# Two fused transformer layers on one core: steps spread over batches by TensorE's work, a gate chunk ahead of attention, meta tokens in one product, first keys in two parts

## The chip, the core and the metric

One core of a Trainium2 chip runs the whole program in one launch. The metric is the device time of that launch in microseconds (us), over several runs. Engines are named as in the profile: PE (TensorE), PEld (its weight loads), DVE (VectorE), ACT (ScalarE), POOL (GpSimd), SP (SyncE, which issues the plain DMAs). All arithmetic is float32.

## What is computed

Two layers over 512 tokens of width 1024, 16 learned meta tokens ahead of them in the first layer. In short:

```python
a = rmsnorm([meta, x], w)                       # 528 rows
aq, ak, av, rq, rf, ri, rg = split(a @ w_in)    # 7 x 512 columns
att = diff_attention(aq, ak, av)                # 4 heads, 2 softmaxes each, causal
rec = hgrn2(rq, rf, ri, rg)                     # gated recurrence, 4 heads, gated by silu(rg)
h = x + [att, rec] @ w_out
# per token: 8 heads; scores against 2 x 128 keys, top 16 of the 16 x 16 sums -> 128 experts
hid = gelu(u_table[experts] @ rmsnorm(h)) * softmax(scores)
h = rmsnorm(h + hid @ v_table[experts])
# second layer: stick-breaking attention (8 heads) and a spatial gate, gated sum, w_out, norm
```

A pair of expert rows (one of `u`, one of `v`) is 2 x 4 KB; 512 tokens x 128 experts make 537 MB of gathers, beside 201 MB of weights and inputs.

## The kernel before

**Blocks.** The tokens are four blocks of 128. The first layer's mixing runs for blocks (0), (1) and (2, 3); the second layer for (0, 1), (2) and (3).

**Gathers and batches.** POOL issues 512 indirect DMAs (line 1804), each of 128 pairs of rows (1.05 MB), into a ring of eight buffers `uv_rows`. A batch ("tick") is two gathers; there are 256, 64 to a block. In each, DVE multiplies the u halves with the tokens (`dots`, line 1618, two instructions), ACT applies gelu (`gelu`), DVE makes the weights (`mix`, lines 1627 and 1628), and PE adds the weighted v halves into the two banks `py` (`rows`: 4 products in the program, 8 records in the trace). Only `rows` frees the two buffers (`uv_free`), for which POOL waits. The ring is thus four ticks deep.

**Order of the work.** `make_plan` writes one list of steps, PLAN, and every engine walks it in order, doing its part of each step. First comes all that block 0 needs before its first gather (`first`), then the 256 ticks, then block 3's second layer. Into the ticks, `spread` deals the rows of the other blocks' work: row r of n goes to tick `lo + r * (hi - lo) // n`, whatever it costs. A row is a list of steps that stand together: of projections two tiles (one where the group has two blocks), of attention one stage each of two heads (`pipeline`). In PE's list `rows` of tick k-1 stands behind the steps of tick k.

**Steps that matter here.** `rf`, `rq`, `ak`, `aq` are tiles of a product with columns as the result (`cols_tile`: 8 products, 512 KB of weights); `ri`, `av`, `rg`, `out` and most of the second layer have rows as the result (`rows_tile`: 4 tiles to a chunk, whose PSUM banks stay open until the fourth). `wq` (4 tiles) and `sc` make the scores of two heads of the expert lookup, `tk` is their top-16 on DVE in six parts. Attention of a head: `us` (scores), `ue` (exponentials on ACT), `uw` (weights on DVE), `ut` (transposes), `uv` (values). `lx`, `ly`, `lm` are the levels of the recurrence: DVE differences and ACT exponentials, DVE products, PE products. `zs` to `zv` are the second layer's attention, `zb` and `za` its gates. PSUM: three banks `pa`, three `pb`, two `py`. Weights go through four slots `wbuf`, loaded by SP in PLAN's order as slots come free (`load_tile`).

**Keys before.** For heads 2i, 2i+1 of block b, `keys` puts the five steps at one tick, 5 ahead of the need, and hands out up to two or four a tick where no chunk is open and no scores wait.

**Meta tokens before.** For group (0) the 16 meta columns lie in `aT_meta`, apart; `cols_tile` makes 8 products of 128 columns and then 8 of 16 columns for the tiles of `rf` and `ak`.

**Constants before.** SP issues x, the angles, meta and 15 constants ahead of the first weights; all constants count on one semaphore `ld_c`, for which `rows_to_columns(0)`, `lambdas` and `norm1` wait.

Of the kernel before, what the change touches and what calls it, by code (L numbers as in the profile page):

```python
# [14 lines left out]
P = 128  # L15
D = 1024
# [97 lines left out]
def mixing_rows(g):  # L114
# [4 lines left out]
    if g == (0,):  # L119
        rows[0].append(("lam",))  # L120
# [4 lines left out]
    rows += second + [[("fq", g)]]  # L125
    proj = tiles("ri", g) + tiles("ak", g) + tiles("av", g) + tiles("aq", g)
# [4 lines left out]
    else:  # L131
# [24 lines left out]
def key_steps(b, i):  # L156
    return [("wq", b, i, t) for t in range(4)] + [("sc", b, i)]
# [67 lines left out]
def use(s):  # L225
# [12 lines left out]
    if name in ("ua", "ud"):  # L238
# [5 lines left out]
            "xt": (2, 0, 0), "sc": (1, 0, 1), "n3": (0, 2, 0), "zs": (0, 1, 0), "zt": (1, 0, 0), "zv": (1, 0, 0),  # L244
# [28 lines left out]

def make_plan():
# [11 lines left out]
    keys = {}  # L286
    for b in range(NB):
        for i in range(4):
            slot = PER_HEAD * (HP * b + 2 * i - LEAD)
            if slot > 0:  # L290
                keys[slot - 5] = ([("xt", b)] if (b, i) == (3, 0) else []) + key_steps(b, i)
    out, pending, chunk = [], [], Open()
    for k in range(n):
# [6 lines left out]
        pending += keys.get(k, [])  # L300
        room = 2 if len(pending) > 2 else 4
        for s in [None] + ticks[k]:
            if s:
                out.append(s)
                chunk.add(s)
            while pending and room and not chunk.now():
                out.append(pending.pop(0))
                room -= 1
# [4 lines left out]
    assert not pending  # L313
# [54 lines left out]
def build(nc, t, out):  # L368

    ctx = ExitStack()  # L370
    with ctx:
# [113 lines left out]
        aT_meta = cut(aT_words[:, KT * P:KT * P + KT * NM], KT, NM)  # L485
# [111 lines left out]
        def _(sp):  # L597
# [38 lines left out]
            for s in PLAN:  # L636
# [28 lines left out]
                if use(s)[2]:  # L665
                    load_tile()
# [1249 lines left out]
```

## Time and profile before

| | us |
|---|---|
| median of 3 runs | 2182.97 (2171.31 to 2190.44) |
| profiled execution, its own time | 2175.92 |
| its span | 2174.1 |
| PE busy | 1750.3 (81%) |
| DVE busy | 1323.0 (61%) |
| ACT busy | 640.2 (29%) |
| POOL busy | 574.5 (26%) |

The span is the time from the first to the last instruction of the profiled execution; 1.8 us of its time lie around it. Busy shares are means over stages that differ: there are no gathers in the first 205 us nor in the last 160, and in between PE is busy all of some stretches and little over half of others. Bytes moved in a stretch, in GB/s, tell how near the transfers are to what they reach elsewhere in the same execution.

### The profile page before, as it was taken

Reading aid. Unit: us, or ns where it says so; the run is one execution under the profiler, and the core shown is the slowest. Engines: PE = TensorE matmul, PEld = TensorE weight load, DVE = VectorE, ACT = ScalarE, POOL = GpSimd, SP = SyncE. Lnnn points to the kernel's source line nnn. Section 1 sums busy time; section 2 is a strip of 40 time slices with the busy share of each in tenths; the row PEclk is TensorE's granted clock in tenths of the full one; section 3 lists DMA queues with packets and bytes.
Section 4 is the critical chain, followed back from the end, with each engine's and each line's share of the span. In section 5 each row is a group of like instructions: output and inputs, shape, how many; then the busy total and the mean of one; then the engine's idle time right before and its main releaser. Section 6 shows DMA issues by size and latency. Waiting matters only on the chain.

```text
span 2174.1 us, 20766 instructions
## 1 busy us (share of the span) xinstructions
PE 1750.3 (81%) x7102; PEld 883.9 (41%) x7102; DVE 1323.0 (61%) x3450; ACT 640.2 (29%) x1233; POOL 574.5 (26%) x516
## 2 busy tenths in 40 slices
PE   7975788768898786887565999889996886777897
PEld 5744454316464342433122635353434342222553
DVE  2324678766778646667777457766566577744231
ACT  3121423322443233302014113621213145311361
POOL 0001224332322222224443222333333333422000
PEclk9977899888999877797886999899997997999899
DMA  5426999998998756699999999899999999999665
GB/s 177 145 64 217 377 411 415 372 417 342 412 394 332 277 227 259 262 418 393 421 420 363 379 397 374 315 355 417 416 379 401 417 416 400 387 417 412 216 212 183
DMA packets 132906, 739.59 MB, mean 340 GB/s; under 512 B 15793, under 2 KB 17201, under 8 KB 67265
## 3 DMA queue, kind: packets, MB, share of 16 engines
q0 software_dynamic: 73728, 536.90, 61.1%
q1 hardware_dynamic: 59072, 201.36, 25.1%
q8 instruction: 57, 0.93, 0.2%
q14 instruction: 49, 0.39, 0.1%
HBM read 736.11 MB, written 2.10 MB: 340 GB/s over the span
## 4 chain that ended last, share of the span: by engine, by line
PE 48%; DMA 28%; DVE 13%; ACT 5%; issue 4%; POOL 2%; SPq 0%; POOLq 0%; DVEq 0%
PE pa L695 28%; DMA uv_rows<-in_peer_uv,small 17%; DMA wbuf<-in_wt 11%; PE py L695 10%; PE pb L695 8%; DVE uv_rows L1618 4%; POOL uv_rows L1804 2%; ACT area L1057 2%; ACT L1053 1%; DVE small L1527 1%; ACT an L1057 1%; DVE tk L1628 1%; DVE small L1605 1%; PE pb L731 1%; ACT small L1057 0%
## 5 line engine op out<-in xcount | busy, mean ns | idle before, releaser
L1804 POOL DMA_INDIRECT uv_rows<-in_peer_uv,small x512 | 574.3, 1122 | 1428.8 <-PE py L695 1135.3
L1618 DVE CUSTOM_DVE_ANT_0 uv_rows<-uv_rows,xrep 128x1024 f32<-128x1024 f32 x512 | 617.5, 1222 | 299.6 <-DMA uv_rows<-in_peer_uv,small 299.1
L695 PE MATMUL py<-uv_rows,tk 128*64 128x512 f32 x2048 | 575.3, 690 | 135.1 <-DVE tk L1628 134.7
L695 PE MATMUL pa<-wbuf,area 128*128 128x512 f32 (+1 forms) x800 | 377.7, 616 | 45.8 <-DMA wbuf<-in_wt 31.6
L1057 ACT ACTIVATE small<-small 128x2 f32<-128x2 f32 (+3 forms) x324 | 69.1, 214 | 1003.4 <-DVE small L1618 993.2
L695 PEld LDWEIGHTS py<-uv_rows,tk 128*64 128x64 f32 x2048 | 138.8, 152 | 459.7 <-issue 251.8
L695 PEld LDWEIGHTS pa<-wbuf,area 128*128 128x128 f32 (+1 forms) x800 | 144.0, 191 | 264.8 <-issue 209.2
L695 PE MATMUL pa<-area,wbuf 128*128 128x128 f32 (+2 forms) x1280 | 202.5, 317 | 8.1 <-DMA wbuf<-in_wt 4.6
L695 PEld LDWEIGHTS pa<-area,wbuf 128*128 128x128 f32 x1280 | 180.7, 199 | 40.0 <-issue 18.6
L695 PE MATMUL pb<-wbuf,area 128*128 128x512 f32 x352 | 168.1, 622 | 22.9 <-DMA wbuf<-in_wt 15.1
L1057 ACT ACT_TABLE_LOAD x137 | 175.8, 1283 | 28.4 <-PE pa L695 20.0
L1057 ACT ACTIVATE area<-pa 128x512 f32<-128x512 f32 (+7 forms) x227 | 87.0, 406 | 221.6 <-PE pa L695 205.2
L695 PE MATMUL pa<-xnT,wbuf 128*128 128x128 f32 x1024 | 130.3, 287 | 25.6 <-DMA wbuf<-in_wt 8.5
L1053 ACT ACT_TABLE_LOAD x101 | 129.6, 1283 | 62.9 <-DVE area L1420 47.0
L695 PEld LDWEIGHTS pa<-xnT,wbuf 128*128 128x128 f32 x1024 | 123.7, 200 | 50.3 <-issue 31.2
L695 PE MATMUL pa<-area 128*128 128x128 f32 (+7 forms) x408 | 99.6, 383 | 39.1 <-ACT area L1057 26.6
L695 PEld LDWEIGHTS pb<-wbuf,area 128*128 128x128 f32 x352 | 65.3, 195 | 123.3 <-issue 82.1
L695 PEld LDWEIGHTS pa<-area 128*128 128x128 f32 (+2 forms) x408 | 66.3, 231 | 79.8 <-ACT area L1057 41.3
L695 PE MATMUL pb<-area 128*128 128x128 f32 (+7 forms) x434 | 79.6, 324 | 3.3 <-DVE area L1431 1.4
L1628 DVE TENSOR_TENSOR tk<-small,tk 128x128 f32<-128x128 f32 x256 | 74.9, 293 | 8.9
L1627 DVE TENSOR_TENSOR tk<-small 128x2 f32<-128x2 f32 x256 | 41.1, 161 | 61.1 <-PE py L695 41.0
L1057 ACT ACTIVATE area<-area 128x512 f32<-128x512 f32 (+3 forms) x104 | 67.4, 655 | 19.4 <-DVE area L1420 14.4
(198 smaller groups left out, 1195.0 us busy)
## 6 DMA issues: line engine op xcount, KB each, us to landing
wbuf<-in_wt SPq DMA_DIRECT2D x352, 512.0 KB, 7.9
uv_rows<-in_peer_uv,small POOLq DMA_INDIRECT x512, 11.3
wbuf<-in_skT SPq DMA_DIRECT2D x16, 256.0 KB, 7.3
h<-in_x SPq DMA_DIRECT2D x4, 512.0 KB, 11.6
fw<-in_finw SPq DMA_DIRECT2D x4, 512.0 KB, 11.3
out<-h SPq DMA_DIRECT2D x4, 512.0 KB, 6.0
an<-in_x SPq DMA_DIRECT2D x3, 512.0 KB, 6.1
uv_rows<-in_finw SPq DMA_DIRECT2D x2, 512.0 KB, 6.0
```

The lines of the kernel that those rows point to most:

```text
L695: return nc.tensor.matmul(o, l, r, start=start, stop=stop, skip_group_check=True)
L731: last = nc.tensor.transpose(ps[:, P * k:P * (k + 1)], src[:, P * (4 * h + k):P * (4 * h + k + 1)], ident)
L1053: nc.scalar.preload_act_table_set("natural_log_exp_and_others")
L1057: return nc.scalar.activation(dst, src, func, **more)
L1527: last = V.tensor_reduce(mx[:, q, part:part + 1], psum_a[(first + part) % RA][:, 0:nk - lo], AXX, ALU.max)
L1605: V.tensor_scalar(gate[to, cols], gexps[tok, g % 2, s_::TG], gsum[tok, g % 2, 1:2], None, ALU.mult)
L1618: last = V.tensor_tensor_reduce(uv_rows[:, n % RING, 0:D], uv_rows[:, n % RING, 0:D], xrep[:, b % 2, n % TG, :], 1.0, 0.0, ALU.mult, ALU.a ...
L1627: step(V.tensor_tensor(wcol[:, k % 2, :], dots[:, at:at + BATCH], gate[:, col:col + BATCH], ALU.mult))
L1628: V.tensor_tensor(mix_w[k % 2], token_mask.unsqueeze(1).broadcast_to([P, BATCH, TOK]), wcol[:, k % 2, :].unsqueeze(2).broadcast_to([P, BAT ...
L1804: nc.gpsimd.indirect_dma_start(uv_rows[:, n % RING, :], None, t["peer_uv"], bass.IndirectOffsetOnAxis(ap=expert_ids[:, c:c + 1].bitcast(U3 ...
```

## The change

1. **Spread by work.** `spread` weighs each row by `tensor_work` (at least `LEAST` = 2) and places its middle in proportion; no two rows share a tick while there is room. The ranges are a little longer: blocks 2 and 3's mixing by 4 ticks, the second layer of (0, 1) ends 4 ticks later.
2. **Keys placed one by one.** `place_keys` walks each key step through a window of up to 16 ticks ahead of its need and takes the tick with least PE work in which no chunk is open and no scores wait.
3. **Gate chunk.** For (2, 3) the four tiles of `rg` stand ahead of attention, not in its first two rows.
4. **Meta tokens.** The 16 meta columns lie behind the 128 in one operand; a tile of `rf` or `ak` is 8 products of 144 columns.
5. **First keys in two parts.** For heads 0 and 1 `sc` becomes two steps `s1`, each behind two `wq`, and `tk` of head 0 waits for the first alone.
6. **Constants.** Only `ident` and `normw` are loaded ahead of the weights, on a semaphore of their own; the others and the angles follow the fourth `rf` tile; `lam` stands with the first `rq` row.

```diff
@@ mixing_rows
-    second[0] = second[0] + [("fs", g)]
+    second[0] = second[0] + [("lam",)] * (g == (0,)) + [("fs", g)]
...
-        rows += weave(chain, proj) + [[("rotq", g)]]
+        rows += weave(chain, proj) + [[("rotq", g)] + rg[0:1]] + pairs_of(rg[1:], n)
...
-    att[0] = att[0] + rg[0:1]
-    att[1] = att[1] + rg[1:4]
+    if len(g) == 1:
+        att[0] = att[0] + rg[0:1]
+        att[1] = att[1] + rg[1:4]
@@ key_steps
+    if (b, i) == (0, 0):
+        return [s for h in range(2) for s in (("wq", b, i, 2 * h), ("wq", b, i, 2 * h + 1), ("s1", b, i, h))]
@@ spread
-    for r, row in enumerate(rows):
-        ticks[lo + r * (hi - lo) // len(rows)] += row
+    work = [max(LEAST, sum(map(tensor_work, row))) for row in rows]
+    done, at = 0, lo - 1
+    for row, w in zip(rows, work):
+        at = min(at + 1, lo + int((done + w / 2) * (hi - lo) / sum(work)))
+        ticks[at] += row
+        done += w
@@ place_keys
+            lo = max(last, inputs_at.get(b, 0) + 1, need - 2 * PER_HEAD + 1)
+            for j, s in enumerate(steps):
+                end = lo + max(1, (need - lo) // (len(steps) - j))
+                spots = [k for k in range(lo, end) if gaps[k]] or [k for k in range(lo, len(ticks)) if gaps[k]][:1]
+                k = min(spots, key=lambda k: work[k])
@@ make_plan
-    spread(mixing_rows((2, 3)) + input_rows(2) + [[("xt", 2)]], q3, PER_BLOCK + q3, ticks)
+    spread(mixing_rows((2, 3)) + input_rows(2) + [[("xt", 2)]], q3, PER_BLOCK + q3 + 4, ticks)
-    spread(second_rows((0, 1)), 2 * PER_BLOCK + 6, 3 * PER_BLOCK + 10, ticks)
-    spread(second_rows((2,)), 3 * PER_BLOCK + 10, n, ticks)
+    spread(second_rows((0, 1)), 2 * PER_BLOCK + 6, 3 * PER_BLOCK + 14, ticks)
+    spread(second_rows((2,)), 3 * PER_BLOCK + 14, n, ticks)
@@ sync
+                if s == ("rf", (0,), 3):
+                    for name, dst in CONSTS:
...
+                    load_angles((0,))
@@ cols_tile
-                    last = mm(ps[:, 0:n], w[:, k, :], src[:, k, :], k == 0, k == KT - 1)
-                for k in range(KT if meta is not None else 0):
-                    last = mm(ps[:, n:n + NM], w[:, k, :], meta[:, k, :], k == 0, k == KT - 1)
+                    last = mm(ps[:, 0:n], w[:, k, :], src[:, k, 0:n], k == 0, k == KT - 1)
```

On PE, at the start of the program (behind the transposes of the inputs): the last two `rf` tiles, `rq` and the first `ri` tile, before

```order
L695 MATMUL pa<-area,wbuf 128x128 x8
L695 MATMUL pa<-area,wbuf 128x16 x8
L695 MATMUL pa<-area,wbuf 128x128 x8
L695 MATMUL pa<-area,wbuf 128x16 x8
L695 MATMUL pa<-area,wbuf 128x128 x32
L695 MATMUL pa<-wbuf,area 128x512 x2
L695 MATMUL pa<-wbuf,area 16x512 x2
```

and now, from the transposes on:

```order
L800 MATMUL pb<-ident,uv_rows 128x16 x8
L788 MATMUL pb<-ident,an 128x128 x8
L754 MATMUL pa<-area,wbuf 128x144 x32
L754 MATMUL pa<-area,wbuf 128x128 x32
L754 MATMUL pa<-wbuf,area 128x512 x2
L754 MATMUL pa<-wbuf,area 16x512 x2
```

The 32 products of 16 columns of `rf` are gone, and its 32 products of 128 columns have 144.

On PE, where attention of block 2 begins (`pa<-area 128x400` are scores, `pa<-wbuf,area 128x512` tiles of `rg`, `xnT` a `wq` tile, `py` is `rows`), before

```order
L695 MATMUL pb<-area 128x512 x2
L695 MATMUL py<-uv_rows,tk 64x512 x4
L695 MATMUL pa<-area 128x400
L695 MATMUL pa<-tri,ident 128x128
L695 MATMUL pa<-area 128x400
L695 MATMUL pa<-tri,ident 128x128
L695 MATMUL pa<-wbuf,area 128x512 x4
L695 MATMUL py<-uv_rows,tk 64x512 x4
L695 MATMUL pa<-wbuf,area 128x512 x12
L695 MATMUL pa<-xnT,wbuf 128x128 x16
L695 MATMUL py<-uv_rows,tk 64x512 x4
L695 MATMUL pa<-xnT,wbuf 128x128 x16
```

and now

```order
L754 MATMUL pb<-area 128x512 x2
L754 MATMUL pa<-wbuf,area 128x512 x4
L754 MATMUL py<-uv_rows,tk 64x512 x4
L754 MATMUL pa<-wbuf,area 128x512 x4
L754 MATMUL py<-uv_rows,tk 64x512 x4
L754 MATMUL pa<-wbuf,area 128x512 x4
L754 MATMUL py<-uv_rows,tk 64x512 x4
L754 MATMUL pa<-wbuf,area 128x512 x4
L754 MATMUL py<-uv_rows,tk 64x512 x4
L754 MATMUL pa<-area 128x400
L754 MATMUL pa<-tri,ident 128x128
L754 MATMUL pa<-area 128x400
```

One `rg` tile stands between two `rows` where three stood with two `wq` tiles, and the scores follow the chunk.

On PE, at the `zb` chunk of the second layer of (0, 1), before

```order
L695 MATMUL pa<-xnT,wbuf 128x128 x16
L695 MATMUL pa<-wbuf,area 128x512 x8
L695 MATMUL py<-uv_rows,tk 64x512 x4
L695 MATMUL pa<-wbuf,area 128x512 x4
L695 MATMUL py<-uv_rows,tk 64x512 x4
L695 MATMUL pa<-wbuf,area 128x512 x4
L695 MATMUL pa<-xnT,wbuf 128x128 x16
```

and now

```order
L754 MATMUL pa<-wbuf,area 128x512 x4
L754 MATMUL py<-uv_rows,tk 64x512 x4
L754 MATMUL pa<-ident,xrep 128x64 x16
L754 MATMUL pa<-xnT,wbuf 128x128 x8
L754 MATMUL pb<-area 128x64 x16
L754 MATMUL py<-uv_rows,tk 64x512 x4
```

The tiles of the chunk stand one to a tick, without key steps; ahead of the attention that follows there now stand `xt` (`ident,xrep`), one `wq` and `sg` (`pb<-area 128x64`) in one tick, where before it `za`'s four tiles stood in one.

## Rows read from the trace of the kernel before

**Rows 1.** The page, part 2: GB/s in 40 equal slices of the span.
```profile
GB/s 177 145 64 217 377 411 415 372 417 342 412 394 332 277 227 259 262 418 393 421 420 363 379 397 374 315 355 417 416 379 401 417 416 400 387 417 412 216 212 183
```

**Rows 2.** Windows where the second layer's tiles already stand one a tick.
```profile
1250.00:1275.00 25.00, 25.00 (x72) 9.02 (x71) 16.48 (x47) 4.88 (x10) 7.61 (x8) 1.00 1.02 419
```

**Rows 3.** Windows: us; busy of PE, PEld, DVE, ACT, POOL; clock; DMA share; GB/s.
```profile
234.00:500.00 266.00, 211.47 (x964) 109.61 (x963) 195.01 (x524) 82.88 (x165) 85.84 (x78) 0.88 0.98 400
500.00:725.00 225.00, 201.52 (x926) 117.91 (x928) 174.41 (x463) 81.63 (x134) 72.66 (x66) 0.94 0.94 368
725.00:775.00 50.00, 37.51 (x138) 19.02 (x140) 19.47 (x48) 10.46 (x21) 7.55 (x7) 0.80 0.67 249
775.00:900.00 125.00, 87.87 (x291) 40.36 (x292) 79.07 (x220) 42.89 (x108) 29.95 (x27) 0.71 0.57 214
...
1175.00:1275.00 100.00, 93.77 (x379) 52.84 (x378) 59.10 (x168) 19.41 (x45) 26.89 (x28) 0.94 0.94 371
1275.00:1475.00 200.00, 180.04 (x720) 89.23 (x719) 132.95 (x329) 78.03 (x130) 58.40 (x53) 0.92 0.91 355
1475.00:1825.00 350.00, 299.15 (x1136) 132.81 (x1136) 230.98 (x612) 97.01 (x184) 116.01 (x100) 0.95 1.00 409
```

**Rows 4.** Timeline of the first keys: `wq` and `sc` on PE, top-16 on DVE, first gather.
```profile
183.59 9.05 PE L695 MATMUL pa<-xnT,wbuf 128*128 128x128 f32 x64 [0.69 <-ACT xnT L1057]
193.00 1.16 PE L695 MATMUL pa<-wbuf,qp 128*128 128x128 f32 x8 [0.37 <-ACT qp L1057]
...
194.83 0.29 DVE L1566 MAX8 tk<-sc 128x8 f32<-128x128 f32 x1 [21.23 <-ACT sc L1057]
...
205.62 1.07 POOL L1804 DMA_INDIRECT uv_rows<-in_peer_uv,small  x1 [205.17 <-DVE small L1606]
```

**Rows 5.** Timeline of PE and POOL where the `rg` chunk runs: start, us, [idle before].
```profile
744.10 6.73 PE L695 MATMUL pa<-wbuf,area 128*128 128x512 f32 x8 [8.27 <-ACT area L1057]
...
752.63 10.57 PE L695 MATMUL pa<-wbuf,area 128*128 128x512 f32 x24
...
752.98 0.94 POOL L1804 DMA_INDIRECT uv_rows<-in_peer_uv,small  x1 [22.62 <-PE py L695]
...
763.03 3.73 PE L695 MATMUL pa<-xnT,wbuf 128*128 128x128 f32 x32
```

**Rows 6.** Timeline of PE around the `za` chunk of the second layer.
```profile
1343.11 1.94 PE L695 MATMUL py<-uv_rows,tk 128*64 128x512 f32 x8
...
1348.22 13.90 PE L695 MATMUL pa<-wbuf,area 128*128 128x512 f32 x32
1362.05 1.94 PE L695 MATMUL py<-uv_rows,tk 128*64 128x512 f32 x8
```

**Rows 7.** Windows of `py` alone (x counts its records, 8 a tick), attention of blocks 2, 3.
```profile
775.00:909.00 134.00, 40.26 (x128) 9.66 (x128) 0.00 (x0) 0.73 0.60 227
```

**Rows 8.** Timeline inside that attention, one head of block 3.
```profile
861.05 1.29 DVE L1527 TENSOR_REDUCE small<-pa 128x1 f32<-128x512 f32 x2 [4.59 <-PE pa L695]
...
868.38 0.20 ACT L1057 ACTIVATE small<-small 128x2 f32<-128x2 f32 x1 [10.05 <-DVE small L1618]
...
870.82 0.37 PE L830 MATMUL pa<-ident,area 128*16 128x128 f32 x1 [7.94 <-ACT area L1057]
```

**Rows 9.** Groups by shape, PE, 17.5 to 101 us (x records, two to a product | busy us, mean ns).
```profile
L695 PE MATMUL pa<-area,wbuf 128*128 128x128 f32 x248 | 31.9, 287 | 0.9 <-DVE area L1380 0.9
...
L695 PE MATMUL pa<-area,wbuf 128*128 128x16 f32 x128 | 15.3, 261 | 0.0
```

**Rows 10.** Timeline of the start: PE's first wait, then two levels of the recurrence.
```profile
13.34 1.03 PE L743 MATMUL pb<-ident,uv_rows 16*128 16x16 f32 x8 [13.34 <-DMA small<-in_bs]
...
57.23 2.05 PE L695 MATMUL pb<-area 128*128 128x128 f32 x16
...
64.20 0.42 DVE L1431 TENSOR_TENSOR area<-area 128x256 f32<-128x256 f32 x1
...
69.76 2.03 PE L695 MATMUL pb<-area 128*128 128x128 f32 x16
```

More of the change, by code:

```diff
@@ L271, in add, with place_keys @@
             self.scores = s[0] == "us"
+def place_keys(ticks):
+    chunk, gaps = Open(), []
+    for row in ticks:
+        free = [] if chunk.now() else [0]
+        for i, s in enumerate(row):
+            chunk.add(s)
+            free += [] if chunk.now() else [i + 1]
+        gaps.append(free[:1])
+    work = [sum(map(tensor_work, row)) for row in ticks]
+    inputs_at = {s[1]: k for k, row in enumerate(ticks) for s in row if s[0] == "xt"}
+    inputs_at[0] = 0
+    chosen, last = [[] for _ in ticks], 0
+    for b in range(NB):
+        for i in range(4):
+            need = PER_HEAD * (HP * b + 2 * i - LEAD) - 1
+            if need < 0:
+                continue
+            steps = ([("xt", b)] if (b, i) == (3, 0) else []) + key_steps(b, i)
+            lo = max(last, inputs_at.get(b, 0) + 1, need - 2 * PER_HEAD + 1)
[3 more added lines that the diff above has]
+                k = min(spots, key=lambda k: work[k])
+                chosen[k].append(s)
+                work[k] += tensor_work(s)
+                lo = k
+            last = lo
+    for k, steps in enumerate(chosen):
+        if steps:
+            ticks[k][gaps[k][0]:gaps[k][0]] = steps
 def make_plan():
@@ L281, in make_plan @@
     spread(mixing_rows((1,)) + input_rows(1) + [[("xt", 1)]], 0, q3, ticks)
-    spread(mixing_rows((2, 3)) + input_rows(2) + [[("xt", 2)]], q3, PER_BLOCK + q3, ticks)
+    spread(mixing_rows((2, 3)) + input_rows(2) + [[("xt", 2)]], q3, PER_BLOCK + q3 + 4, ticks)
     spread([[("ldpost",)], *input_rows(3), [("ldfin1",)]], 2 * PER_BLOCK, 2 * PER_BLOCK + 5, ticks)
-    spread(second_rows((0, 1)), 2 * PER_BLOCK + 6, 3 * PER_BLOCK + 10, ticks)
-    spread(second_rows((2,)), 3 * PER_BLOCK + 10, n, ticks)
[L286 to L292, printed above, removed]
+    spread(second_rows((0, 1)), 2 * PER_BLOCK + 6, 3 * PER_BLOCK + 14, ticks)
+    spread(second_rows((2,)), 3 * PER_BLOCK + 14, n, ticks)
+    place_keys(ticks)
+    out = []
     for k in range(n):
@@ L299, in make_plan @@
             out.append(("take", b - 1))
[L300 to L308, printed above, removed]
+        out += ticks[k]
         g = k // PER_HEAD + LEAD
@@ L710, in rows_tile @@
                     open_banks.clear()
-                    open_banks.extend(bank() for _ in range(len(g) + (meta is not None)))
+                    open_banks.extend(bank() for _ in range(len(g) + meta))
                 for j, ps in enumerate(open_banks):
@@ L717, in rows_tile @@
                         else:
-                            last = mm(ps[0:NM, :], meta[:, 2 * i + k, :], w[:, k, :], i + k == 0, i == n_tiles - 1 and k == 1)
+                            last = mm(ps[0:NM, :], src[:, k0 + 2 * i + k, P * len(g):], w[:, k, :], i + k == 0, i == n_tiles - 1 and k == 1)
                     if i == n_tiles - 1:
@@ L735, in rows_to_columns @@
                 if b == 0:
[L736 removed]
+                    pe.wait_ge(ld_i, LOADED_F)
                     rows[0] += 1
@@ L865, in key_scores, with head_scores @@
                 last.then_inc(a_full, 1)
+            def head_scores(b, i, h):
+                pe.wait_ge(a_free, A_AT[("wq", b, i, 2 * h + 1)])
+                sk = cut(tile()[:, 0:2 * P], 2, P)
+                ps = a_bank()
+                for k in range(2):
+                    last = mm(ps[:, P * k:P * (k + 1)], qp[:, 2 * h + k, :], sk[:, k, :], True, True)
+                last.then_inc(a_full, 1)
             def weighted_rows(k):
@@ L1277, in _ @@
                     empty(qp[:, s[3], :], bank()[:, 0:P])
+                elif name == "s1":
+                    empty(sc[:, 0, 2 * P * s[3]:2 * P * (s[3] + 1)], bank()[:, 0:2 * P])
                 elif name == "sc":
```

76 lines of the change are left out of this document (49 added, 27 removed).

## The prediction

> **What bounds the kernel now.** I read the bytes per slice first, then the stretches one by one, then the timeline where a stretch falls short.
>
> The slices show a plateau: 15 of the 33 between the first and the last gather stand at 400 to 421 GB/s, and a valley of five stands at 227 to 332 [rows 1]. A stretch of 25 us at 419 GB/s has a DMA share of 1.02, that is, the transfers are never idle there [rows 2]. I take 418 GB/s as what the transfers reach. What a stretch misses of it is time in which they had nothing to do, and as the bytes are fixed (537 MB of gathers, 201 MB besides), only that time can be won between the gathers. It is us x (1 - GB/s / 418) [rows 3]:
>
> - 234 to 500: 266 x 18/418 = 11.5 us
> - 500 to 725: 225 x 50/418 = 26.9 us
> - 725 to 775: 50 x 169/418 = 20.2 us
> - 775 to 900: 125 x 204/418 = 61.0 us
> - 1175 to 1275: 100 x 47/418 = 11.2 us
> - 1275 to 1475: 200 x 63/418 = 30.1 us
> - 1475 to 1825: 350 x 9/418 = 7.5 us
>
> Together 168 us. The other part is the start, where no gather runs until 205.6 us [rows 4]: there PE and the chains between engines set the pace.
>
> Why the transfers pause: a gather needs a free buffer, and only `rows` frees one. The longest waits of POOL are for `py` (22.6 us before the gather at 753) [rows 5]. So a tick in which PE, in its order, does long work ahead of `rows` empties the ring of four ticks.
>
> **The change, part by part.**
>
> *Gate chunk.* At 744.1 PE runs the first `rg` tile at the lower clock (6.7 us), one `rows`, then three tiles (10.6 us) and two `wq` tiles (3.7 us) ahead of the next `rows` [rows 5]. From 744 to 767 the ring gets two buffers back in 23 us. Before that the first tile waited 8.3 us for the exponentials to free a bank. In the changed order one tile (10.57 / 3 = 3.5 us) stands between two `rows` (1.9 us [rows 6]): 5.4 us a tick, under the (2.10 + 0.52 MB) / 418 = 6.3 us that a tick's transfers take. Of 20.2 us I leave 3 for the entry of the chunk: **-17**. Bounds: 0 (the wait at `us20` stays and merely moves) and -20.
>
> *Attention of blocks 2 and 3.* From 775 to 909, 128 records of `py` are 16 ticks in 134 us, 8.4 us a tick, against 2.10 / 418 = 5.0 us for the gathers of one [rows 7]. The cause is a chain, not work: DVE's maxima wait 4.6 us for PE's scores, ACT's gelu waits 10.1 us for the dots behind them, PE's transposes wait 7.9 us for the exponentials, and `rows` stands behind these [rows 8]. The change leaves this chain as it is. But its 18 rows lie in 18 ticks (79 to 96), where they lay in 17 (74 to 90), with four `wq` and one `sc` among them (2.36 MB). If the chain takes its 134 us again, it hides 18 x 2.10 + 2.36 = 40.1 MB where 134 x 227 GB/s = 30.4 MB passed: 9.7 MB, 23 us. The key steps each take a bank and an ACT copy inside the chain, so I take **-21**. Bounds: 0 (each key step lengthens the chain by what it hides) and -45 (the higher clock, since PE idles less, also shortens the scores).
>
> *Second layer of (0, 1).* The four `za` tiles and the scores keep two `rows` 19 us apart (1343.1 to 1362.1; the four tiles alone are 13.9) [rows 6]; `zb` shares its ticks with key steps just before. Now tiles stand one to a tick up to 159, but `xt`, one `wq` and `sg` share tick 160, and `za` comes in pairs. Of 30.1 us **-13**. Bounds -4 and -26. The 11.2 us from 1175 on belong to the norms (`n1` to `n3`), a chain that the change leaves: 0.
>
> *Mixing of (2, 3) and (1).* Two thirds of the 26.9 us lie where `wq` and `ak` tiles share ticks 59 to 61 (about 10 us of work where DVE's levels wait as well); the rest is the expert input of block 1, unchanged. **-10**, bounds -2 and -18. In 234 to 500 the keys move to earlier ticks: **-3**, bounds 0 and -6. From 1475 on the stretches are near the plateau: 0.
>
> *Meta tokens.* 128 records of 16 columns take 15.3 us, 0.120 each, as much as one of 128 columns (31.9 / 248 = 0.129) [rows 9]: such a product costs its weight load, whatever its width. They go, and 128 records grow by an eighth of 0.12, +1.9 us: -13.4 on a PE that is busy without a gap from 19 to 101 us. What is late next is the recurrence: from the start of one level's products (57.2) to the last input of the next (64.6) 7.4 us pass, and PE came to the next level at 69.8 with three `ak` tiles between [rows 10]. These shrink by 5.0 us, so it comes at 64.8, just behind the chain. I take 1.4 us off for this and for `lam`, whose exponentials now stand ahead of the sigmoids: **-12**. Bounds -6 and -13.
>
> *Constants.* PE's first product waited until 13.3 us for the last constant [rows 10]; the normed x, made by a chain on ACT, is late next. That chain starts with meta's landing, whose DMA now goes out two issues earlier. **-2**, bounds 0 and -5. SP passes 15 more issues (13 constants, 2 angles) ahead of the first `rq` tile, whose slot only comes free with the first `rf` tile: nothing waits.
>
> *First keys.* The top-16 started at 194.8, behind four `wq` and one `sc` [rows 4]. Now two `wq` and half of an `sc` stand ahead: 9.05 / 2 + 0.6 = **-5**, for the first gather and, since DVE then runs both heads through without a wait, for the dots. Bounds -2 and -6.
>
> The sum: start -12 - 2 - 5 = -19; gathers -17 - 21 - 13 - 10 - 3 = -64. The profiled execution took 2175.92, so 2092.9; the median of the runs stands 7 us above it, so **2100 us** (-3.8%).
>
> **A rule on the transfers.** The rows say 418 GB/s [rows 2, 3]. The Trainium skill, "DMA: Bandwidth & Descriptors", section "Specifications", gives an HBM limit of some 358 GB/s per core. By that figure the plateau could not exist and the stretches at 355 to 371 would be full; it would cancel the gains there, as the first rival below has it by another way; the trace disagrees with it by 60 GB/s.
>
> **The rivals.**
>
> *The transfers are the bound already (2164 us, 0.10).* If the pauses are only the transfers' own unevenness, time won in one stretch is lost in the next, and the start alone counts: 2183 - 19 = 2164. For it: four of the seven stretches run at 0.94 or more of a share [rows 3]. Against it: shares of 0.57 and 0.67 in the valley, with POOL waiting for `py` [rows 3, 5].
>
> *The attention chain eats its share (2141 us, 0.21).* Each of the five key steps between the scores of two heads lengthens the chain: a `wq` waits for a bank, its copy stands in the same row of ACT's work as the exponentials, and its products take 1.9 us at the higher clock (two tiles in 3.73 [rows 5]) and twice that at the lower, 4 us a step. Then the -21 is 0 and 20 us come on top: 2100 + 41 = 2141. For it: the chain is one wait after the other [rows 8] and the granted clock there is 0.71 [rows 3].
>
> *The clock falls where work is thinned (slower, 0.05).* Place: the second layer of (0, 1), 69 ticks (137 to 205), now 3.5 + 1.9 = 5.4 us of PE each at 2.4 GHz, with pauses between where the kernel before was busy throughout. At 1.2 GHz a tick is 10.8 us, 4.5 over the transfers' 6.3. From 83 / 4.5 = 18 such ticks on, all gain is gone; with 40 of them, 2183 - 83 + 180 = 2280 us. For it: the granted clock was 0.71 where PE was busy for 70%. Against it: one tile a tick ran at 1.00 [rows 2], and a slower PE is a busier one, which gets its clock back. The Trainium skill, "TensorE: Matmul & The Clock Gate", Part 1, says that pauses bring back the lower clock; the trace agrees in the valley.
>
> **How the numbers follow.** Forecast 0.64, attention rival 0.21, transfers 0.10, clock 0.05. The likeliest has its own range, 2075 to 2125. With the outer bounds of the gathers (24 us more from the attention, 24 from the other four) less some that cannot all come true, the low end is 2062; the high end, 2150, takes in the attention rival. A change under 1% can't be told from none. The transfers rival lies at that border (2161), half on each side: faster 0.64 + 0.21 + 0.05 = 0.90, same 0.05, slower 0.05.
>
> **What would show it.** The first gather near 187 us instead of 205.6, and no record of 16 columns on `pa<-area,wbuf`. No wait of POOL for `py` above 15 us where the `rg` chunk runs. Attention of blocks 2 and 3 over 18 ticks in 134 us at some 300 GB/s. The `za` chunk with `rows` at most 12 us apart. A granted clock near 1.00 from 1200 to 1500. I am wrong if the valley keeps its depth (attention), if it is gone and others appear (transfers), or if the second layer shows a clock under 0.8.

## Result and profile after

| | before | changed |
|---|---|---|
| median | 2184.5 us (2171.31 to 2190.44, 4 runs) | 2148.12 us (2142.02 to 2151.48, 4 runs) |
| ratio, 95% interval | | 0.986 (0.9813 to 0.9907) |
| profiled execution / span | 2175.92 / 2174.1 | 2142.02 / 2140.2 |
| PE busy | 1750.3 | 1727.3 |

The kernel is 1.4% faster where 3.8% was forecast. The time lies inside the range, near its upper end, and the gain is under half of what was said. The two profiled executions differ by 33.9 us, and I follow those, stretch by stretch.

The page of the changed kernel, part 2, GB/s in 40 slices:

```profile
GB/s 201 142 95 268 386 417 415 367 416 344 383 412 338 416 366 244 276 420 355 421 419 318 418 418 309 303 351 414 418 418 346 415 416 364 378 417 405 218 210 183
```

Beside [rows 1] the deep valley has shrunk from five slices to two (244 and 276). Further on it is worse than before: 355 and 318 stand where it was 393 and 363, 309 and 303 where it was 374 and 315, and 346 where it was 401.

To compare the same work, each stretch runs from one stage's first step to the next one's. PLAN says in which tick a stage begins, and as `rows` of tick k-1 stands behind the steps of tick k, the stage begins where `rows` of two ticks earlier ends. Windows of the changed kernel, cut so, with the columns of [rows 3]:

```profile
219.00:482.00 263.00, 213.35 (x953) 108.01 (x954) 195.11 (x522) 80.53 (x161) 87.67 (x79) 0.87 0.99 402
482.00:719.00 237.00, 213.66 (x1007) 128.17 (x1006) 182.61 (x488) 86.07 (x144) 76.44 (x69) 0.94 0.94 374
719.00:897.00 178.00, 130.73 (x488) 59.92 (x486) 124.86 (x336) 59.20 (x142) 52.35 (x46) 0.82 0.81 314
897.00:1107.00 210.00, 155.63 (x606) 67.58 (x604) 148.38 (x401) 39.01 (x88) 83.51 (x72) 0.83 0.98 398
1107.00:1144.00 37.00, 12.72 (x42) 5.26 (x40) 18.14 (x47) 16.95 (x28) 8.00 (x7) 0.63 0.79 317
1144.00:1310.00 166.00, 155.13 (x605) 77.92 (x603) 107.65 (x281) 34.16 (x72) 52.74 (x49) 0.97 0.98 397
1310.00:1409.00 99.00, 80.63 (x335) 41.12 (x334) 70.35 (x176) 51.44 (x82) 25.38 (x24) 0.85 0.77 285
1409.00:1621.00 212.00, 200.19 (x686) 81.50 (x684) 138.91 (x375) 39.37 (x84) 75.41 (x66) 0.99 1.01 415
1621.00:1982.00 361.00, 268.42 (x960) 107.55 (x960) 215.98 (x528) 111.23 (x200) 110.01 (x96) 0.89 0.96 390
```

and of the kernel before (its first stretch is that of [rows 3], 234 to 500 at 400 GB/s):

```profile
500.00:727.00 227.00, 203.37 (x932) 118.30 (x932) 175.67 (x466) 81.63 (x135) 73.42 (x66) 0.94 0.94 369
727.00:922.00 195.00, 142.43 (x532) 70.48 (x532) 112.83 (x303) 60.93 (x144) 45.03 (x40) 0.75 0.64 244
922.00:1153.00 231.00, 160.06 (x564) 59.70 (x564) 167.93 (x456) 38.88 (x89) 92.72 (x80) 0.82 1.00 413
1153.00:1181.00 28.00, 13.85 (x42) 4.22 (x40) 19.31 (x49) 11.70 (x21) 10.15 (x8) 0.63 0.97 387
1181.00:1345.00 164.00, 152.61 (x609) 81.24 (x609) 99.85 (x265) 39.81 (x79) 43.76 (x42) 0.96 0.96 380
1345.00:1438.00 93.00, 79.72 (x322) 40.63 (x320) 73.37 (x182) 46.24 (x74) 29.30 (x26) 0.85 0.86 328
1438.00:1643.00 205.00, 193.79 (x662) 80.46 (x660) 127.96 (x344) 43.52 (x87) 67.90 (x60) 0.99 0.98 394
1643.00:2015.00 372.00, 282.37 (x1064) 119.01 (x1064) 229.20 (x565) 114.22 (x208) 118.19 (x104) 0.92 1.00 407
```

With the prediction's own formula, us x (1 - GB/s / 418), the transfers' missed time is:

| stage | first tick, before / changed | missed before, us | missed now, us | change | forecast |
|---|---|---|---|---|---|
| block 1, to the mixing of (2, 3) | 0 / 0 | 11.5 | 10.1 | -1.4 | -3 |
| mixing of (2, 3) | 41 / 41 | 26.6 | 24.9 | -1.7 | -10 |
| gate chunk and attention of (2, 3) | 74 / 75 | 81.2 | 44.3 | -36.9 | -38 |
| `out` and expert inputs, to the norms | 94 / 98 | 2.8 | 10.0 | +7.2 | 0 |
| norms of (0, 1) | 134 / 134 | 2.1 | 8.9 | +6.8 | 0 |
| products of (0, 1), `q2` to `zb` | 138 / 137 | 14.9 | 8.3 | -6.6 | -13 for this and the next two |
| `za` and attention of (0, 1) | 159 / 161 | 20.0 | 31.5 | +11.5 | |
| `ga` to `wo` of (0, 1) | 172 / 173 | 11.8 | 1.5 | -10.3 | |
| second layer of block 2, to the last gather | 202 / 206 | 9.8 | 24.2 | +14.4 | 0 |
| sum | | 180.7 | 163.7 | -17.0 | -64 |

The time from the first `rows` to the last fell by 18 us, which agrees. The start gave 15 us more (first `rows` at 218.9 instead of 233.9), the work behind the last gather 0.7.

**The start.** Timeline of the changed kernel, first keys:

```profile
166.82 5.48 PE L754 MATMUL pa<-xnT,wbuf 128*128 128x128 f32 x32 [0.69 <-ACT xnT L1123]
173.83 0.29 DVE L1634 MAX8 tk<-sc 128x8 f32<-128x128 f32 x1 [16.99 <-ACT sc L1123]
181.50 0.69 DVE L1664 TENSOR_REDUCE tk<-tk 128x32 f32<-128x512 f32 x1
187.38 0.60 ACT L1123 ACTIVATE sc<-pa 128x512 f32<-128x512 f32 x1 [1.25 <-PE pa L754]
188.01 0.22 ACT L1123 ACTIVATE tk<-tk 128x16 f32<-128x16 f32 x1
188.42 0.16 DVE L1666 RECIPROCAL tk<-tk 128x1 f32<-128x1 f32 x1 [6.23 <-ACT tk L1123]
190.14 1.08 POOL L1872 DMA_INDIRECT uv_rows<-in_peer_uv,small  x1 [189.69 <-DVE small L1674]
```

Against [rows 4], `wq` starts 16.8 us earlier, the top-16 21.0 us earlier, the first gather only 15.5. Between the two DVE waits 6.2 us for ACT, whose exponentials of the top-16 stand in its list behind the copies (`qp`, `sc`) of the keys of heads 2 and 3. Before, DVE reached that place at 203.2 us and the last of the copies ended at 203.5, so the wait was 0.7 us.

**The gate chunk**, timeline of PE:

```profile
725.83 3.70 PE L754 MATMUL pa<-wbuf,area 128*128 128x512 f32 x8
729.46 1.94 PE L754 MATMUL py<-uv_rows,tk 128*64 128x512 f32 x8
731.33 3.70 PE L754 MATMUL pa<-wbuf,area 128*128 128x512 f32 x8
734.96 1.94 PE L754 MATMUL py<-uv_rows,tk 128*64 128x512 f32 x8
736.83 3.70 PE L754 MATMUL pa<-wbuf,area 128*128 128x512 f32 x8
740.46 1.94 PE L754 MATMUL py<-uv_rows,tk 128*64 128x512 f32 x8
```

One tile and one `rows` in 5.5 us (the forecast said 5.4), against the 23 us for two `rows` in [rows 5].

**The second layer's attention**, timeline of PE, the last heads of (0, 1):

```profile
1366.19 0.70 PE L754 MATMUL pb<-area 64*128 64x256 f32 x2
...
1370.96 0.65 PE L969 MATMUL pa<-ident,area 128*128 128x128 f32 x4 [2.62 <-ACT area L1123]
1371.55 3.49 PE L754 MATMUL py<-uv_rows,tk 128*64 128x512 f32 x8
...
1382.40 1.12 PE L969 MATMUL pa<-ident,area 128*128 128x128 f32 x4 [4.14 <-ACT area L1123]
1383.44 2.91 PE L754 MATMUL py<-uv_rows,tk 128*64 128x512 f32 x8
...
1393.32 1.12 PE L969 MATMUL pa<-ident,area 128*128 128x128 f32 x4 [5.93 <-ACT area L1123]
1394.36 3.68 PE L754 MATMUL py<-uv_rows,tk 128*64 128x512 f32 x8
```

Here one `rows` comes every 11 us: each tick holds a full turn of the chain (scores `zs`, exponentials `ze` on ACT, transposes `zt`, for which PE waits 2.6 to 5.9 us). The granted clock is 0.85 over this attention, and `rows` itself takes 2.9 to 3.7 us here where it took 1.9 beside the gate chunk. Before, attention of (0, 1) had 12 ticks in 78 us (1345 to 1423), now it has 11 in 90 (1310 to 1400).

### The profile page after: what moved, and what is told of

Its sections match the earlier page's. It is cut to its first block, busy times and chain, and to the rows that moved or that the text cites. A ratio compares the mean times of both kernels' runs of the same rounds, so it can differ in the third digit from the quotient of the medians.

```text
span 2140.2 us, 20511 instructions
## 1 busy us (share of the span) xinstructions
PE 1727.3 (81%) x6974; PEld 864.4 (40%) x6974; DVE 1324.3 (62%) x3450; ACT 638.4 (30%) x1233; POOL 579.7 (27%) x516
## 4 chain that ended last, share of the span: by engine, by line
PE 30%; DMA 17%; DVE 9%; ACT 4%; issue 2%; POOL 1%; POOLq 0%; DVEq 0%; SPq 0%
PE pa L754 15%; DMA uv_rows<-in_peer_uv,small 10%; PE py L754 8%; DMA wbuf<-in_wt 6%; PE pb L754 6%; DVE uv_rows L1686 3%; ACT area L1123 1%; ACT L1119 1%; POOL uv_rows L1872 1%; DMA fw<-in_finw 1%; ACT an L1123 1%; DVE area L1750 1%; DVE tk L1696 0%; PE pb L788 0%; ACT small L1123 0%
## 5 line engine op out<-in xcount | busy, mean ns | idle before, releaser
L1123 ACT ACTIVATE small<-small 128x2 f32<-128x2 f32 (+4 forms) x324 | 69.1, 214 | 1051.0 <-DVE small L1686 1027.1
L754 PE MATMUL pa<-area,wbuf 128*128 128x128 f32 (+2 forms) x1152 | 183.7, 317 | 4.9 <-DMA wbuf<-in_wt 3.1
L754 PE MATMUL pb<-wbuf,area 128*128 128x512 f32 x352 | 168.7, 622 | 20.6 <-DMA wbuf<-in_wt 10.2
L1123 ACT ACT_TABLE_LOAD x139 | 178.3, 1283 | 14.9 <-PE pa L754 6.9
L754 PEld LDWEIGHTS pa<-area,wbuf 128*128 128x128 f32 x1152 | 162.6, 194 | 37.1 <-issue 21.9
L754 PEld LDWEIGHTS pa<-xnT,wbuf 128*128 128x128 f32 x1024 | 123.9, 199 | 44.3 <-issue 38.3
L754 PE MATMUL pa<-area 128*128 128x128 f32 (+7 forms) x408 | 89.7, 354 | 31.3 <-ACT area L1123 27.0
L754 PEld LDWEIGHTS pa<-area 128*128 128x128 f32 (+2 forms) x408 | 60.6, 213 | 76.3 <-issue 34.0
L1123 ACT ACTIVATE area<-area 128x512 f32<-128x512 f32 (+3 forms) x104 | 67.4, 655 | 17.9 <-DVE area L1488 12.9
L788 PE MATMUL pb<-ident,an 128*128 128x128 f32 x56 | 13.8, 428 | 69.4 <-ACT an L1123 69.4
```

The lines of the kernel that those rows point to most:

```text
L754: return nc.tensor.matmul(o, l, r, start=start, stop=stop, skip_group_check=True)
L788: last = nc.tensor.transpose(ps[:, P * k:P * (k + 1)], src[:, P * (4 * h + k):P * (4 * h + k + 1)], ident)
L1123: return nc.scalar.activation(dst, src, func, **more)
```

## The experiments

A tick is two gathers, which take 5.0 us where nothing holds them. The expectations name theories by letters; the one that matters most is **theory T**: a stage bound by its chain of waits between engines takes its own time, however many ticks lie under it; every tick laid there is carried for nothing, and every tick taken from it costs 5 us elsewhere. The version before was timed beside each group of runs: 2174.22 us with the first four, 2178.28 with the next four, 2176.07 with the next four, 2175.22 with the last two, single runs 2164 to 2196. Ratios are to it.

**1. The parts alone.**

e1_gate is the kernel before with the gate chunk ahead of attention:

```diff
-        rows += weave(chain, proj) + [[("rotq", g)]]
+        rows += weave(chain, proj) + [[("rotq", g)] + rg[0:1]] + pairs_of(rg[1:], n)
```

> The kernel before with the gate chunk of (2, 3) ahead of attention and nothing else. Theory A (the gain between the gathers is the gate chunk's alone, and the spread by PE's work gives part of it back): the stretch that missed 81 us between 725 and 900 misses some 47, as in the changed kernel, so 28 to 35 us less, ratio 0.984 to 0.987. Theory B (the gain is the spread's, the chunk's place matters little): under 10 us, ratio above 0.995. Theory C (time won in one stretch is lost again in the next, as the transfers are uneven by themselves): about 15 us, ratio 0.993, with new pauses after 900.

2168.42 us, ratio 0.9978 (0.9948 to 1.0007). No gain that can be told from none. Its trace is of the fastest of its 12 runs (2157.34), and there the gate chunk and attention of (2, 3) (720 to 906, 276 GB/s) miss 63.2 us (186 x 142/418), 18 less than before.

e2_start is the kernel before with the start's edits (meta tokens, constants, first keys, `lam`).

> The kernel before with the meta tokens in one product, the constants behind the first tiles, lam moved and the first keys in two parts; spread, keys, gate chunk as before. All theories: the first weighted rows end at 219 instead of 234 us, and nothing later moves: 15 us less, ratio 0.993. Theory C differs after that: the shift need not reach the end, 5 to 15 us.

2156.28 us, ratio 0.9913 (0.9873 to 0.9953): -18 us. In its trace the first `rows` ends at 221.1 us, 12.7 earlier than before and not the 15 that was expected.

e3_start_gate has both.

> The start's edits and the gate chunk, with spread, ranges and keys of before. Theory A: both add up, 45 to 50 us less, ratio 0.978, which is 12 or more below the changed kernel. Theory B: 20 us less at most, ratio 0.991. Theory C: as the changed kernel, ratio 0.985.

2149.7 us, ratio 0.9885 (0.9844 to 0.9925): -24.5 us, about the two added (18 + 6).

e4_old_spread is the changed kernel with `spread` and the ranges of before:

```diff
-    work = [max(LEAST, sum(map(tensor_work, row))) for row in rows]
-    done, at = 0, lo - 1
-    for row, w in zip(rows, work):
...
+    for r, row in enumerate(rows):
+        ticks[lo + r * (hi - lo) // len(rows)] += row
```

> The changed kernel with rows dealt by their index and the ranges of before; keys placed one by one, gate chunk ahead, start as changed. Theory A (spread by PE's work gives back time because rows light on PE are packed together though chains between engines bound them): 10 to 20 us faster than the changed kernel, ratio to before 0.976 to 0.980. Rival K (the key steps placed into the second layer's attention are what gives back): no faster than the changed kernel, 0.985. Rival S (the spread is a gain of its own, hidden by the keys): slower than it, 0.99.

2134.67 us, ratio 0.9815 (0.9779 to 0.985). All its runs (2129 to 2138) lie below all ten of the changed kernel (2140 to 2151, with e5_again below), but on another chip; by the ratios the gap is 5 to 10 us and their intervals overlap, so alone it only suggests that the spread by work, the centre of the change, costs time. e9_after_ranges below decides it. The keys placed one by one are worth about 15 us (e3 to e4) under the old spread.

**2. What is wrong with the spread.**

e5_again is the changed kernel once more, beside the next three.

> The changed kernel as it is, on the same chip as the next three. All theories: 0.986 to the kernel before, within its interval; it is the base for the others.

2142.57 us, ratio 0.9838 (0.98 to 0.9876).

e6_no_gate has the gate chunk back in attention's first rows.

> The changed kernel with the rg tiles of (2, 3) back in the first two rows of attention. Theory T (attention of (2, 3) is bound by its chain, and the chunk costs its 18 to 20 us of PE in either place; what counts is the number of ticks laid under it): 3 to 8 us slower than the changed kernel. Theory G of the prediction (the chunk inside attention empties the ring and costs 17 us on its own): 15 to 20 us slower.

2161.41 us, ratio 0.9921 (0.9892 to 0.995): 19 us slower than e5_again. The 15 to 20 us of theory G held here, the 3 to 8 of theory T did not. Chunk and attention (first product to last) take 164 us in e6_no_gate over 19 ticks, and 20 + 146 = 166 us over 22 ticks in e5_again. The time of the stage is the same and three more ticks fit under it, 15 us: T's own arithmetic, which I had applied wrongly. So T and G name the same 15 us here, and this run does not separate them. The missed time of chunk and attention is 61.9 us here (725 to 914, 281 GB/s: 189 x 137/418), against 81.2 before and, by the same cut, 46.2 in e5_again: of the forecast's -38, some 15 are the chunk's place and some 20 the attention's, close to the -17 and -21 said.

`rows` of tick 78 ends 20 us later than in e5_again, of tick 90 33 us later, and 11 to 15 us of it stay to the end.

e7_least4 changes a number:

```diff
-LEAST = 2
+LEAST = 4
```

> The changed kernel with LEAST 4 in place of 2: rows that are light on PE weigh more, so the second layer's attention has 14 ticks for (0, 1) and 16 for (2), where it has 11 and 14. Theory T (a chain-bound stage takes its own time, so each tick laid under it saves up to 5.0 us of the transfers' pace elsewhere): 8 to 15 us faster than the changed kernel, about e4. Rival P (such a stage takes a fixed time per tick, 8 us, since each tick's handshakes bound it, so ticks given to it cost as much as they save): no change, within 3 us.

2117.51 us, ratio 0.9719 (0.9678 to 0.9759): 25 us faster than e5_again, more than the 8 to 15 of theory T. Rival P (no change) is out.

e8_chain gives the rows of chains a weight of their own:

```diff
+CHAIN = {"us": 5, "ue": 5, "zs": 4, "zd": 4, "n1": 5, "n2": 4, "x2": 4, "x3": 4}
...
-    work = [max(LEAST, sum(map(tensor_work, row))) for row in rows]
+    work = [row_work(row) for row in rows]
```

where `row_work` is the largest of the row's chain weight, `LEAST` and its sum of `tensor_work`.

> The changed kernel with weights for rows of attention (5 and 4), norms and expert inputs (4 and 5), which gives the attentions 19, 14 and 17 ticks (18, 11 and 14) and takes them from the product stages. Theory T: 12 to 20 us faster than the changed kernel, 2125 to 2135, at or below e4. Rival P: no change, or slower by some us where (2, 3) has 19 ticks.

2102.39 us, ratio 0.9659 (0.9614 to 0.9703): 40 us faster than e5_again. The direction is T's and rival P falls, but T had said 12 to 20 us: its arithmetic was half of what came.

**3. Which chain.** The same version with a part of the weights each, and the placing by number in the changed kernel's ranges.

> The changed kernel with a weight of 5 for the first attention's rows alone (us, ue). It gets 19 ticks instead of 18 for blocks 2 and 3, and the mixing ahead of it 30 instead of 31. Theory T (a stage bound by its chain carries ticks for nothing, each worth 5.0 us elsewhere): one tick, so 5 us off, a time of 2135 to 2145. Rival S (the 40 us came from smoothness in general, the sum is not divided by stages): each of the three part versions takes most of the 40 us, so about 2110 to 2120 here.

2141.07 us, ratio 0.9821 (0.9785 to 0.9857).

> The changed kernel with a weight of 4 for the second layer's attention rows alone (zs, zd). (0, 1) gets 15 ticks for it instead of 11, block (2) 18 instead of 14. Theory T: 8 ticks under chains, 5.0 us each but not all of them won since the attention of (0, 1) was not wholly idle: 20 to 35 us off, 2110 to 2125, and the missed time of 1300 to 1425 us of the changed kernel (37 us) falls below 20. Rival S: about the same time as the other part versions.

2118.23 us, ratio 0.9723 (0.9686 to 0.9761).

> The changed kernel with weights of 5 for n1 and 4 for n2, x2, x3 alone (norms and expert input). The norms of (0, 1) get 5 ticks instead of 3, x2 and x3 no longer share one; but the second layer's attentions get one tick fewer each (10 and 13). Theory T: 2 to 3 ticks gained under the norms and the expert input (10 to 15 us), 2 lost under the attentions (5 to 10 us): 0 to 10 us off, 2135 to 2148. Rival S: 2110 to 2120, as the others.

2145.51 us, ratio 0.9846 (0.9808 to 0.9883).

> The changed kernel with its longer ranges, but rows placed by their number again, as before. The attentions of the second layer get 13 and 17 ticks, the norms 5, the attention of blocks 2 and 3 18. Theory T: close to the version that knows the chains, since by number a chain's rows weigh as much as any: 2110 to 2130. If the longer ranges alone are what costs (rival R), it is slower than the index version with the ranges of before (2134.7): 2140 to 2150.

2124.66 us, ratio 0.9746 (0.9709 to 0.9784).

All four medians fall where theory T put them; rival S (each takes most of it) and rival R (the longer ranges cost) are out. The last of the four is the plainest test of the spread: only the rule of `spread` differs from the changed kernel, it is 18 us faster than e5_again, and the intervals of the two ratios do not touch. So the spread by work costs time.

The second layer's attentions alone give 24 us of the 40, the first attention's tick 1.5 (less than the 5 expected, and inside the spread of runs), the norms' weights nothing by themselves. The traces show why: against e5_again, e12_chain_nx misses some 21 us less in the head of the mixing of (2, 3) and in the norms of (0, 1) and of block 2, but 14 us more in block 2's attention, which has a tick less, and 5 more behind it. Together the three give some 17 us more than their sum: with weights on the attentions too, what the norms gain is no longer paid there. The longer ranges are 10 us to the good by the medians of e4 and e9, with intervals that overlap slightly.

The attention of (0, 1), first product to last, in the changed kernel (11 ticks):

```profile
1310.00:1400.00 90.00, 73.93 (x305) 38.39 (x306) 61.59 (x155) 46.98 (x73) 22.81 (x22) 0.85 0.75 277
```

in e11_chain_zs (15 ticks):

```profile
1296.00:1387.00 91.00, 82.45 (x386) 43.59 (x384) 77.94 (x190) 51.47 (x83) 33.60 (x29) 0.92 0.95 373
```

and in e8_chain (14 ticks):

```profile
1286.00:1379.00 93.00, 77.23 (x328) 38.52 (x326) 75.07 (x191) 50.18 (x79) 30.14 (x27) 0.89 0.87 336
```

The stage takes 90, 91 and 93 us; what differs is what passes under it, 277, 373 and 336 GB/s. That its time is its own holds among these versions, not in general: in the kernel before it took 78 us with 12 ticks. Read from the ends of `rows`, it took 79 to 80 us in before and e1 to e3, where no key step stands in it, 84 in e4, with the same 12 ticks and four key steps, and 89 to 95 in the versions with the changed ranges and 10 to 15 ticks. The attention of block 2 took 91 us with 14 ticks in the changed kernel, 95 with 17 in e8 and 101 with 18 in e11: there a tick costs 1 to 3 us of its own, still less than the 5 it saves elsewhere. The 101 us that it took with 13 ticks in e12 are not explained. At 277 GB/s 30.4 us of transfers are missed (90 x 141/418), at 373 GB/s 9.8 (91 x 45/418): 20 of the 24 us stand in this one stretch. In the window 1300 to 1425 e12_chain_nx (second line), with a tick fewer under the chain, has less than the changed kernel (first line):

```profile
1300.00:1425.00 125.00, 105.94 (x452) 54.43 (x453) 83.37 (x206) 53.86 (x88) 33.09 (x31) 0.88 0.80 298
1300.00:1425.00 125.00, 104.80 (x433) 53.18 (x432) 79.60 (x195) 53.62 (x87) 32.16 (x30) 0.86 0.75 278
```

POOL's waits from 1275 to 1425 (waited for: us in total, times, longest), in the kernel before (first line) and the changed one

```profile
POOL uv_rows L1804 <- PE py L695: 95.0, 18, 16.0
POOL uv_rows L1872 <- PE py L754: 104.8, 17, 10.2
```

and in e11_chain_zs:

```profile
POOL uv_rows L1881 <- PE py L763: 95.3, 23, 9.9
```

The longest wait does not rank the three: it fell from 16.0 to 10.2 us in the changed kernel, which lost time here, and hardly differs in e11, which won it. The mean does: 5.3 us before, 6.2 in the changed kernel, 4.1 in e11.

**4. The 5.5 us lost at the start.** e13_tk_ahead is the changed kernel with

```diff
-    first = [...] + key_steps(0, 0) + key_steps(0, 1)
-    for hh in range(LEAD):
+    first = [...] + key_steps(0, 0)
+    first += [("tk", 0, 0, part) for part in range(6)] + key_steps(0, 1)
+    for hh in range(1, LEAD):
```

> The changed kernel with the six parts of the top-16 of head 0 listed ahead of the key products of heads 2 and 3 instead of behind them. In the changed kernel DVE reaches the sums of head 0 at 182.2 us, but ACT's exponentials for them stand in its list behind five copies of those products and start at 188.0. Theory L (that place in ACT's list holds the first gather): ACT waits for DVE instead, the first gather starts at 184 to 185 us instead of 190.1 and the kernel is 4 to 6 us faster (2137 to 2143 beside 2142 to 2148). Rival Q (the first gather is held by DVE's 16 us of work for the head, or what is won is lost when PE, now waiting for ACT's copies, comes late to block 1's mixing): under 2 us of change.

2139.26 us (2136.78 to 2144.42), ratio 0.9832 (0.9786 to 0.9879). Timeline of e13_tk_ahead, ACT's exponentials and the first and ninth gather:

```profile
180.95 0.22 ACT L1124 ACTIVATE tk<-tk 128x16 f32<-128x16 f32 x1 [1.44 <-DVE tk L1656]
184.99 1.07 POOL L1873 DMA_INDIRECT uv_rows<-in_peer_uv,small  x1 [184.54 <-DVE small L1675]
216.19 0.94 POOL L1873 DMA_INDIRECT uv_rows<-in_peer_uv,small  x1 [21.11 <-PE py L755]
```

Now ACT waits for DVE (1.4 us) and not DVE for ACT; the first gather starts 5.2 us earlier, as theory L has it. The ninth, the first that needs a freed buffer, starts 3.0 us earlier (219.2 in the changed kernel), and `rows` of ticks 24 to 66 end some 6 us earlier; of that 1 us is left at tick 90 and 2.6 at the last. The median is 3.3 us below that of e5_again and the ratio 0.0006 (1 us), with intervals that overlap: that ACT's list held the first gather is shown, a gain of the kernel is not.

e14_chain_tk has the same edit on e8_chain.

> The same edit on the version whose spread knows the chains (2102.4 us, ratio 0.966 to before). Theory L: the two add up, 4 to 6 us faster, ratio 0.963 to 0.964, 2095 to 2099 us. Rival Q: no change, ratio 0.966.

2100.48 us (2093.86 to 2102.22), ratio 0.9654 (0.9609 to 0.9699). The first gather starts at 186.4 us; of the 4 to 6 us expected the median shows 1.9, which is no difference that can be told from none. With this the best version is 3.5% faster than before and 2.0% (42 of 2142.6 us) faster than the changed kernel, by ratios that do not touch.

## Why the prediction was right and wrong

**Right: the start, -19.** e2_start gave -18, the profile -15 (first `rows`). By parts: to the first `wq` -16.8 against -14 said (meta tokens and constants); the two shapes of [rows 9] took 47.2 us and take 32.8 now, -14.4 against -13.4; PE's first product came at 11.1 instead of 13.3 us. From `wq` to the top-16 -4.2 against -5. But the first gather came at 190.1, not near 187: I followed the chain through PE, ACT's copy and DVE, and did not look what stands ahead of ACT's next part in it, the exponentials. A chain made shorter on one engine was met by another engine's list; DVE's wait of 0.7 us there in the old trace was the sign that this was next.

**Right: gate chunk and attention of (2, 3), -38.** The windows give -36.9, the tile and `rows` 5.5 us, the attention 18 ticks in 143 us at 291 GB/s, where 134 us and some 300 were said; POOL's longest wait for `py` from 700 to 742 is 5.0 us, under the 15 said. The first rival (transfers the bound already) is out by that valley. The attention rival's 2141 us lies close to the measured time, but by coincidence: it said that the valley keeps its depth, and the valley gave what was forecast, while the misses are elsewhere. Its price of a key step was not tested: the attention's ticks hold five key steps before and now. That they cost something there is suggested by e3 and e4, the same but for the keys: seven stand in the attention's 17 ticks in e3, which take 157 us, five in e4, 142 us.

The same move gave only 5.8 us in the plan of before (e1_gate), with an interval that holds zero. There it leaves seven key steps in the attention, four of them in its first two ticks, and the chunk has 3 ticks where the changed plan has 4; its own trace, of its fastest run, shows the stage 18 us better. How much each of these counts is open.

**Wrong, and the step that failed: the stretches priced at nothing.** The prediction has "a chain that the change leaves: 0" for the norms and "From 1475 on the stretches are near the plateau: 0", and no term for 900 to 1175. These three cost 28.4 us (+7.2, +6.8, +14.4), 28 of the 47 us by which the gathers' gain fell short. The chains were left; their ticks were not: the norms of (0, 1) have 3 instead of 4, the attention of block 2 has 14 instead of 18. `x2` and `x3` of the expert input share a tick of 14.0 us, and `n1` to `n3` of block 2 make one of 22.4 us (each between two ends of `rows` in the timeline). Of the 22.4 us DVE waits 10.1 for the norm's weights `fw`:

```profile
1638.39 1.28 DVE L1835 SCALAR_TENSOR_TENSOR h<-h,small,fw 128x1024 f32<-128x1024 f32 x1 [10.14 <-DMA fw<-in_finw]
```

Their load is listed behind `fd` and `store` of (0, 1), light rows as well, which now share tick 205, right ahead of `n1` in 206. SP issued it at 1623.8; before it issued it at 1637.4, DVE came to the same instruction at 1652.3 and waited 3.2 us, for ACT. Item 1 of the change says that no two rows share a tick while there is room. There was none: 74 rows go into 68 ticks for (2, 3) and 84 into 72 for (0, 1), and those that the new rule lets share are the ones light on PE.

**Half right: the second layer of (0, 1), -13.** By its parts it was -6.6 in the products, -10.3 from `ga` to `wo` and +11.5 in the attention between them, -5.4 in all. One tile to a tick did what was said: the changed kernel's `ga` to `wo` runs at 415 GB/s. The part that failed is "The four `za` tiles and the scores keep two `rows` 19 us apart". I took the missed time there for PE work bundled ahead of `rows`, and forecast `rows` at most 12 us apart as the cure. They are at most 12.9 us apart in the attention now, where two were 18.9 and 15.1 apart before, and the stage misses more: six of its 11 ticks take 10 to 13 us each, twice the 5.0 that their gathers take. What I should have counted was not the longest gap between two `rows` but the stage's time and the ticks under it, before and after: 12 in 78 us and 11 in 90. Cut as in the table it takes 99 us instead of 93 and carries one tick less (5.0 us), which makes the 11.5. The tick is the spread's; for the 6 us, four key steps and a full turn of the chain in each late tick are the likely causes, argued from the order and from e4, not tested alone.

**Wrong: mixing of (2, 3), -10.** It was -1.7. The key steps did leave `ak`'s ticks, and from `ak` on the missed time fell by some 7 us; but ahead of it, it rose by some 5, since rows of the recurrence with little PE work now share ticks: `ri`, `lx` and `ly` stand in one of 14.3 us, where before they had two of 8.6 and 8.1.

So one wrong idea made most of the misses: `tensor_work` counts what PE does, and the new spread gives ticks in that proportion. Products, which need one tick per tile and fill it, get more ticks (`q2` to `zb` 20 to 23, `ga` to `wo` 27 to 32), and the second layer's chains, which keep most of their time whatever lies under them, get fewer. The change took ticks of 5 us from where they are nearly free. The clock rival (0.05) has nothing for it in the products, where a tick was thinned: the granted clock was 0.97 and 0.99 there, 0.96 and 0.99 before; in the attention it was 0.85 in both kernels, where "near 1.00 from 1200 to 1500" was said.

Two slips in the prediction's working change neither its time nor its chances. The outer bounds of the other four parts of the gathers add up to 27 us, not 24, and tiles do not quite stand one to a tick up to 159, since two of `v2` share tick 147. Its sentence that by 358 GB/s "the plateau could not exist" takes the figure for a ceiling of one core that runs alone; see the last section.

**Open.** The keys' own share with the new spread was not tried; only the 15 us under the old one is measured. How much of e1_gate's missing gain is the key steps, how much the shorter chunk and how much the spread of the runs (its 12 runs reach from 2157 to 2180 us) is not settled. The weights of e8_chain are a first guess from the stages' times, and no better ones were looked for.

## What to carry to other kernels

Where one stream (here the gathers) runs beside stages of two kinds, lay it thick under the stages that wait on chains between engines and thin under those that fill the engine: a weight that counts only the bound engine's work does the reverse. Before forecasting a re-spread, write down for every stage its time and its ticks, before and after; a stage that keeps its time and loses n ticks costs up to n times the stream's own pace, also where none of its instructions changed. Cut the stretches of both traces at the same step of the program, not at the same microsecond. And where a chain is shortened on one engine, look in the other engines' lists for what stands ahead of their part in it.

## What the runs showed of the hardware

A product of 144 columns took 0.141 us a record (18.0 us for 128) where one of 128 took 0.116 (14.8 for 128) and one of 16 had taken 0.120: 16 columns cost as much as 128, while 16 columns above 128 cost 0.025, nearly twice the 0.015 (an eighth of 0.12) that I had added. The rows are the groups by shape of the changed kernel, from 14 to 98 us:

```profile
L754 PE MATMUL pa<-area,wbuf 128*128 128x144 f32 x128 | 18.0, 304 | 0.9 <-DVE area L1448 0.9
L754 PE MATMUL pa<-area,wbuf 128*128 128x128 f32 x128 | 14.8, 275 | 0.0
```

Where PE's work for a tick fitted under the transfers, they kept the same rate in all the versions looked at: 419 GB/s in [rows 2], 415 from `ga` to `wo` in the changed kernel, 418 in the same stage of e8_chain (1386 to 1588), and the best slice of both pages is 421. That plateau did not move with the order of the work, which is why the missed time could be added up by stretch. The Trainium skill, "DMA: Bandwidth & Descriptors", section "Specifications", has some 358 GB/s per core as the limit of HBM, and the same page says that this is what each core gets when two cores of an HBM domain stream at once. Here one core runs, and it moved 60 GB/s more: a stretch at 355 to 371 GB/s was not full.
